# The first head's top-16 search of a PEER layer, with its result handed over in two halves of eight

## What is computed

```python
q = jnp.einsum('nd,de->ne', xb, wq).reshape(blk, PEER_HEADS, 2, PEER_HALF)
s = jnp.einsum('nhcd,hckd->nhck', q, keys).astype(jnp.float32)
sv, si = lax.top_k(s, PEER_TOPK)
cand = (sv[:, :, 0, :, None] + sv[:, :, 1, None, :]).reshape(...)
cidx = (si[:, :, 0, :, None] * PEER_N_KEYS + si[:, :, 1, None, :]).reshape(...)
fs, fpos = lax.top_k(cand, PEER_TOPK)
eidx = jnp.take_along_axis(cidx, fpos, axis=-1)
g = jax.nn.softmax(fs, axis=-1)
act = jax.nn.gelu(jnp.einsum('nd,nhkd->nhk', xb, u_tab[eidx]))
return jnp.einsum('nhk,nhkd->nd', (g * act).astype(xb.dtype), v_tab[eidx])
```

## Time and profile before

| | us |
|---|---|
| median of three runs | 1086.61 |
| the three runs | 1085.2, 1086.61, 1089.31 |
| the profiled execution, its own time | 1081.24 |
| its span, first to last instruction | 1079.6 |
| PE busy | 928.7 (86%) |
| DVE busy | 619.8 (57%) |
| POOL busy | 392.8 (36%) |
| mean granted TensorE clock | 0.978 |

### The profile page before, as it was taken

The page is one execution under the profiler, slowest core; times in us unless marked ns, Lnnn a source line. Parts: engine busy times, 40 slices in busy tenths (PEclk is TensorE's granted clock), DMA queues, the critical chain, the costliest instruction groups (busy, mean ns, idle before and its releaser), DMA issues.

```text
span 1079.6 us, 14164 instructions
## 1 busy us (share of the span) xinstructions
PE 928.7 (86%) x4019; PEld 527.8 (49%) x4019; DVE 619.8 (57%) x1593; ACT 346.6 (32%) x1084; POOL 392.8 (36%) x429
## 2 busy tenths in 40 slices
PE   8999989999999998898998998778757777777775
PEld 6886666665677854455564643223221223322222
DVE  0002266661133879767665776888746677677664
ACT  2223244340001242642433433423312342332432
POOL 3320212222100245553443445445434445445440
PEclk9999999999999999999999999999999999999999
DMA  9984588989984799999999999999979999999994
GB/s 334 327 308 173 210 313 283 311 307 368 351 326 163 287 344 420 416 419 394 415 420 356 400 386 412 421 420 420 415 271 423 422 422 421 422 421 422 420 411 187
DMA packets 76094, 387.61 MB, mean 359 GB/s; under 512 B 11440, under 2 KB 14584, under 8 KB 41912
## 3 DMA queue, kind: packets, MB, share of 16 engines
q0 software_dynamic: 46320, 309.65, 71.2%
q1 hardware_dynamic: 25056, 71.34, 18.5%
q10 hardware_dynamic: 4656, 5.86, 1.5%
HBM read 383.74 MB, written 7.27 MB: 362 GB/s over the span
## 4 chain that ended last, share of the span: by engine, by line
PE 47%; DMA 29%; DVE 8%; issue 8%; ACT 4%; POOL 2%; POOLq 0%; SPq 0%; DVEq 0%; ACTq 0%
DMA big<-peer_uv,idx_r 26%; PE ps L1307 17%; PE ps L890 8%; PE ps L950 4%; PE ps L1198 3%; DVE big L1860 3%; DMA ring<-pack_kv 3%; PE ps L928 3%; POOL big L585 2%; PE ps L1162 2%; PE ps L1271 1%; PE ps L1137 1%; PE ps L1183 1%; ACT wts L784 1%; ACT kv_n L788 1%
## 5 line engine op out<-in xcount | busy, mean ns | idle before, releaser
L1307 PE MATMUL ps<-big,kv_n 128*128 128x512 f32 x1024 | 483.1, 617 | 115.3 <-ACT kv_n L788 115.0
L585 POOL DMA_INDIRECT big<-peer_uv,idx_r x264 | 312.8, 1185 | 356.5 <-PE ps L1307 270.3
L1860 DVE CUSTOM_DVE_ANT_0 big<-big,x_n 128x1024 f32<-128x1024 f32 x256 | 312.1, 1226 | 149.6 <-DMA big<-peer_uv,idx_r 145.9
L1307 PEld LDWEIGHTS ps<-big,kv_n 128*128 128x128 f32 x1024 | 190.2, 195 | 379.9 <-issue 197.1
L778 ACT ACTIVATE gel<-dots 128x2 f32<-128x2 f32 x132 | 26.9, 204 | 365.7 <-DVE dots L1860 365.7
L788 ACT ACTIVATE kv_n<-cst,wts 128x128 f32<-128x128 f32 (+1 forms) x264 | 90.8, 391 | 4.3
L890 PE MATMUL ps<-xT_r,ring 128*128 128x264 f32 x368 | 83.9, 392 | 5.1 <-DMA xT_r<-xT 5.1
L890 PEld LDWEIGHTS ps<-xT_r,ring 128*128 128x128 f32 x368 | 71.1, 194 | 17.5 <-DMA ring<-wall 5.0
L784 ACT ACTIVATE wts<-gk,gel 128x1 f32<-128x1 f32 (+1 forms) x256 | 61.4, 287 | 12.4 <-ACT gel L778 0.4
L1198 PEld LDWEIGHTS ps<-xT_r,ring 128*128 128x128 f32 x512 | 61.2, 191 | 7.4 <-issue 7.4
L1198 PE MATMUL ps<-xT_r,ring 128*128 128x128 f32 (+1 forms) x512 | 64.4, 280 | 0.0
(11 more groups left out here) (346 smaller groups left out, 909.3 us busy)
## 6 DMA issues: line engine op xcount, KB each, us to landing
ring<-wall SPq DMA_DIRECT2D x64, 512.0 KB, 6.6
ring<-pack_kv SPq DMA_DIRECT2D x52, 320.0 KB, 5.0
ring<-pack_kv POOLq DMA_DIRECT2D x44, 320.0 KB, 4.9
big<-pack_cmp POOLq DMA_DIRECT2D x42, 128.0 KB, 3.9
pg_r<-pack_kv SPq DMA_DIRECT2D x16, 320.0 KB, 6.2
pg_r<-pack_kv POOLq DMA_DIRECT2D x16, 320.0 KB, 6.2
big<-peer_uv,idx_r POOLq DMA_INDIRECT x264, 10.5
big<-wall SPq DMA_DIRECT2D x2, 2048.0 KB, 11.6
```

The costliest lines, as they stand in the source:

```text
L585: pool.indirect_dma_start(uv_rows[:, slot, :], None, a["peer_uv"], off).then_inc(uv_in[slot], 16)
L1307: return mm(ps[:, 4 + 2 * tt + c, :], at, row, start=False, stop=stop)
L1860: v.tensor_tensor_reduce(out=uv_rows[:, slot, 0:D], in0=uv_rows[:, slot, 0:D], in1=hrow, scale=1.0, scalar=0.0, op0=ALU.mult, op1=ALU.add, ...
```

## The change

A function `look_up(at, done)` is new. It does what parts 5 to 7 of `find` do, but for eight picks: 12 instructions on half the elements, and then it counts a semaphore up. For head 0 of the first group alone, the search now runs parts 0 to 3, looks up picks 0 to 7 and signals the new semaphore `e0_sb`, then runs part 4 and looks up picks 8 to 15 and signals `e_sb`. POOL's first turn waits for `e0_sb`, its second for `e_sb`. All other heads are as before.

```diff
--- before.py
+++ after.py
@@ -358,6 +358,7 @@
         fsub_sb, gexp_sb, e_sb, hs_out, gs_out, es_out, hrep_in, gks_in, eis_in = (
             sem(n) for n in ("fsub_sb", "gexp_sb", "e_sb", "hs_out", "gs_out", "es_out", "hrep_in", "gks_in", "eis_in"))
         idx_st, idx_go = sem("idx_st"), sem("idx_go")
+        e0_sb = sem("e0_sb")
         uv_in = [sem(f"uv_in{i}") for i in range(SLOTS)]
         dot_sb, v_used, gel_sb = sem("dot_sb"), sem("v_used"), sem("gel_sb")
         ss_out, ss_in = sem("ss_out"), sem("ss_in")
@@ -586,10 +587,16 @@
 
             def rows_of_head(tt, h):
 
-                pool.wait_ge(e_sb, found(tt, h))
+                earliest = isinstance(h, int) and found(tt, h) == 1
+                if earliest:
+                    pool.wait_ge(e0_sb, 1)
+                else:
+                    pool.wait_ge(e_sb, found(tt, h))
 
                 pool.sem_inc(idx_go, 1)
                 for i in range(HEAD_T):
+                    if earliest and i == 1:
+                        pool.wait_ge(e_sb, 1)
                     fetch_turn(h * HEAD_T + (turn0(tt, h) + i), i, eidx[:, tt, bass.ds(h * TOPK + i * SLOTS, SLOTS)])
 
             for tt in range(2):
@@ -1841,6 +1848,24 @@
                     own(v.tensor_copy(eidx[0:r, tt, bass.ds(h * TOPK, TOPK)], w.ea[0:r]))
                     dve.sem_inc(e_sb, 1)
 
+            def look_up(at, done):
+
+                w, n = of_prompt, 8
+                io = cst[:, C_IDX:C_IDX + 16].unsqueeze(1).broadcast_to([P, n, 16])
+                oh = w.oneh[:, 0:16 * n].rearrange("p (k i) -> p k i", k=n)
+                for half in range(2):
+                    if half == 0:
+                        own(TS(w.fi[:, 0:n], w.fpos[:, at:at + n], 4, None, ALU.logical_shift_right))
+                    else:
+                        own(TS(w.fi[:, 0:n], w.fpos[:, at:at + n], 15, None, ALU.bitwise_and))
+                    own(v.tensor_copy(w.fif[:, 0:n], w.fi[:, 0:n]))
+                    own(TT(oh, w.fif[:, 0:n].unsqueeze(2).broadcast_to([P, n, 16]), io, ALU.is_equal))
+                    own(TT(oh, oh, w.idf[:, half:half + 1, :].broadcast_to([P, n, 16]), ALU.mult))
+                    own(v.tensor_reduce((w.ea, w.eb)[half][:, 0:n], oh, AXX, ALU.add))
+                own(STT(w.ea[:, 0:n], w.ea[:, 0:n], 128.0, w.eb[:, 0:n], ALU.mult, ALU.add))
+                own(v.tensor_copy(eidx[:, 0, at:at + n], w.ea[:, 0:n]))
+                dve.sem_inc(done, 1)
+
             def normalise(tt, h, count):
 
                 r, c = (P, 0) if tt < 2 else (ROWS_S, 1)
@@ -1894,8 +1919,11 @@
                      {} if tt else {4: (sc0_sb, h * 2 + 6)} if not isinstance(h, int) or h + 2 < NH else {4: (sc_sb, 32)})
 
             dve.wait_ge(sc0_sb, 2)
-            for part in range(8):
+            for part in range(4):
                 find(0, 0, part)
+            look_up(0, e0_sb)
+            find(0, 0, 4)
+            look_up(8, e_sb)
             gate_sum_others(3, 8)
             own(TS(alpha_id, ident, ALPHA, None, ALU.mult))
             dve.wait_ge(ln_in, 64)
```

## The result

| | before | changed |
|---|---|---|
| median, 8 runs each | 1086.09 us | 1092.48 us |
| lowest, highest | 1083.91, 1091.56 | 1087.82, 1094.66 |
| ratio, 95% interval | | 1.0054 [1.0034, 1.0074] |
| profiled execution, own time (span) | 1081.24 (1079.6) | 1089.34 (1087.7) |
| mean granted TensorE clock, profiled execution | 0.978 | 0.981 |

A forecast was written before the change was run, and what follows sets the result against it. The gather stage, a closed loop that becomes DMA's once started, is started by PE's first sum, which DVE's search and merge tiles make late. Split 2.4 + clock 0.7 = +3.1 us on median 1086.61 gives 1089.7, said 1089.5; range 1085 to 1093.5.

The forecast's parts named there:

- The forecast's own span: The likeliest outcome, slower by 2.4 to 4.1 us with 3.1 in its middle, 1087 to 1092 with scatter; chance 0.68.
- the wide range: Range of the time to hold 8 in 10: 1085 to 1093.5 us.
- the case of over 0.5% slower: Whole kernel slower by over 0.5% (5.4 us), needing extra clock cost or the forecast with scatter; chance 0.10.
- Two of its own signs: L1271 on PE at 366.4 to 367.5; second turn's gathers on POOL 2.4 to 3.5 us later.
- Price of an instruction: Look-up instructions on DVE at half width: 0.16 us for 8 elements, 0.29 for 128.
- The split on DVE: Two look-ups of 3.26 us instead of one of 4.11 cost DVE 2.4 us more ahead of the merge tiles.
- The first gathers: POOL's first gather comes 2.8 us earlier, near 357.6, worth nothing because slots 4 to 7 still wait for L1271.
- The waits of PE: PE idle 3.5 us instead of 1.07 ahead of `other_branch(7)`; a half-speed clock stretch follows, costing 0.7 us.
- Hidden work: ACT's table load and exponential, POOL's wait for `e_sb` before its second copy: all hidden, costing nothing.
- The local sum: On the chain through DVE and PE: 2.4 + 0.7 = +3.1 us, against nothing gained.
- The end: The second turn's delay of 2.4 to 3.5 us is kept as the same distance to the end.
- Rival C: Clock costs more: slow stretch wholly on L1271, 1.7, and another 1.7; +5.8 us with the split's 2.4, 1092.4; chance 0.08.

The follow-up runs named there:

- shifted kernel: Changed kernel with 40 more tiny memsets on DVE earlier, in a stretch where DVE waits for PE: 1091.18 us, ratio 1.0058 [1.0031, 1.0086].
- split without early gathers: Changed kernel, but POOL's first turn waits for `e_sb` again, after both look-ups: 1090.6 us, ratio 1.0048 [1.0028, 1.0068].
- six of padding: Kernel before with six more DVE instructions of 128x256, result unused, ahead of the merge: 1089.49 us, ratio 1.0038 [1.0014, 1.0061].
- gathers early, no second look-up: Changed kernel with the second look-up replaced by a copy of the first one's eight numbers and padding: 1087.44 us, ratio 1.0019 [1.0000, 1.0038].
- PE filled: Changed kernel with 24 more matmul calls, output unread, on PE ahead of `other_branch(6)`: 1090.62 us, ratio 1.0048 [1.0031, 1.0066].
- thirteen of padding: Kernel before with thirteen more DVE instructions of 128x256, result unused, ahead of the merge: 1094.29 us, ratio 1.0081 [1.0050, 1.0112].
- merge first: Changed kernel with merge tiles right behind the first look-up, then part 4, second look-up behind mix tiles 2 and 3: 1091.78 us, ratio 1.0063.
- mix tiles first: Changed kernel with merge tiles, mix tiles 0 to 5 and two dots ahead of the second look-up and head 1's search: 1089.35 us, ratio 1.0043.
- fifth dot in the middle: As mix tiles first, but head 0's fifth dot stands between parts 5 and 6 of head 1's search: 1086.28 us, ratio 0.9984 [0.9965, 1.0002].

## Why the prediction was right, and where it was short

The forecast was slower, by 3.1 us, at 1089.5; measured were 5.9 (3.7 to 8.0) and 1092.48, inside the range and 3.0 above the number. The mechanism held in each of its steps, the size was short. The forecast's own span, +2.4 to +4.1 and 1087 to 1092, ends short of 5.9 and 1092.48. That the wide range holds it owes something to the room left there for a slower clock and for scatter, which is luck as much as foresight. The best estimate, 0.54%, lies even in the case of over 0.5% slower that had 0.10. And +3.1 was said to be less than a measurement could tell, while here the comparison is good to 0.2%. Two of its own signs were missed by a little: the output projection starts at 367.7 by the clock of before (366.4 to 367.5 said), and the second turn's gathers are 3.74 us later (2.4 to 3.5 said).

- **Price of an instruction.** 0.17 and 0.29 us, priced at 0.16 and 0.29. The Trainium skill ("VectorE: DVE Perf Modes", section on the TRN2 errata) gives (N + 151)/0.96 ns for a float32 tensor_tensor, which makes an estimate of 0.29 us for 128 elements. The trace agrees with it (0.29 us at L1862).
- **The split on DVE.** +2.4 predicted, +2.90 in the trace. 0.37 of the difference is the gap behind the first look-up (0.61, where the shifted kernel has 0.24); 0.08 is in two small instructions of the second look-up that took 0.20 and 0.22 instead of 0.17. The gap is the part that was mis-sized: the sum of instructions had no place for it. (The shifted kernel, without the gap, pays about as much at two other places.)
- **The first gathers.** 2.8 us earlier predicted, 2.76 measured, worth nothing that shows. Tried twice, by taking only them away and by keeping only them.
- **The waits of PE.** 3.5 us predicted, 3.97 measured. The slow stretch came where it was expected, 0.51 in 364 to 367.5, and cost the path 0.84 where 0.7 was taken.
- **Hidden work.** ACT's table load, POOL's new wait and the landings stayed off the path, as said.
- **The local sum.** +3.1 predicted, 2.90 + 0.84 = +3.74 measured.
- **The end.** That the distance is kept fits, as far as the scatter lets it be read. At the 17th gather it is 3.75 and 3.63 in the two traces. The 264th gather starts 706.97 to 712.10 behind the search before (three traces, mean 709.8) and 714.22 and 715.04 changed, mean 714.6, which is 4.8 later where single traces of one kernel lie 5.1 apart. The padding shows it by the medians. The 8.1 us between the two profiled executions are 0.90 of an earlier start of the search, 3.74 of the change, and 3.5 that lie within what two traces of the same kernel differ.
- **Rival C** gave 1092.4, the time that was measured, but not by its mechanism. It wanted the slow stretch on L1278, or a second one, or more of them later. In both traces there is one such stretch here, L1278 starts behind it (19.91 and 19.79 us behind the search), and the eight executions had a mean granted clock of 0.9784, beside 0.9785 in the 80 executions of the kernel before that the variants were timed against. The near hit is a coincidence as far as the traces go.

What stays between 3.74 (traces) and 5.9 (ratio): the interval just reaches down to 3.74. The variants lie above their local shift in the same way, by their ratios (split without early gathers 5.2 and 3.45, six of padding 4.1 and 3.04, shifted 6.3 and 3.11). Part of this is the clock of the whole execution. Over the 196 runs here whose clock is known, of all kernels, a line fitted through time against granted clock, with a level of its own for each kernel, falls by 0.55 us (0.46 to 0.65) for each 0.001 of clock, and at equal clock the losses are, with 95% bounds:

| | local shift | loss at equal clock |
|---|---|---|
| changed | 3.74 | 4.8 (3.3 to 6.2) |
| split, gathers late | 3.45 | 3.3 (2.0 to 4.6) |
| gathers early, no second look-up | 0.48 | 1.4 (0.2 to 2.7) |
| PE filled | 3.39 | 4.6 (3.0 to 6.1) |
| six of padding | 3.04 | 3.2 (2.0 to 4.5) |
| thirteen of padding | 7.34 | 6.5 (5.0 to 8.0) |
| shifted | 3.11 | 4.6 (3.2 to 6.0) |
| merge first | 3.09 | 2.9 (1.1 to 4.7) |
| mix tiles first | -2.60, then 2.86 at the 17th gather | 3.2 (1.9 to 4.5) |
| fifth dot in the middle | -2.61, then -1.22 at the 17th gather | 1.0 (-0.2 to 2.3) |

Of the first eight, whose shift is read at the first sum, it lies within the bounds in seven and just outside in one (3.11). So the local shift explains a loss to about 1 us. Whether that last microsecond is something the split does later, or chance, is open.

The version with the mix tiles first fits by its 17th gather. The last one leads there by 1.22 us and shows no gain at equal clock, though its ratio alone (-1.7 us, -3.8 to 0.2) would fit. Whether a lead is handed on as a delay is, stays open. (The executions of the kernel before that stood beside the last version were slower than the others, mean 1087.5 for 1086.0 and 1086.1. Against those alone its figure is 0.5, -0.9 to 1.8.) The fit was made after the runs and is no experiment: a kernel in which PE waits more may itself draw a lower clock.

## What to carry to other kernels

An early hand-over is worth only what its receiver is waited for: here the receiver sat in front of a resource that PE held, and the lead turned into idle DMA. Splitting a step to hand over a half costs its fixed instruction times again, on the engine that does it, so look first who else waits for that engine; if it must be split, put the second half behind all that others wait for, and follow the wait to its next place each time, since it moved twice here (mix tiles, fifth dot). Compare two kernels by distances from a common event in the trace, and leave whole spans to the medians.

## What the runs showed of the hardware

- The same two DVE instructions stood 0.61 us apart in one program and 0.24 us apart when 40 instructions more stood ahead of them in the program; about the same time went into two other instructions, 0.19 us each. Splitting or moving code can thus move some 0.4 us to places that no instruction names.
- A wait of PE of 3.83 to 7.05 us in this stretch was followed by half the granted clock in all six traces that have one (0.51 in 364 to 367.5 of the changed kernel), and with PE busy instead it stayed at 1.00. Gaps of 3.13 and 2.79 us were followed by 0.51 and 0.53 in the kernel before and by 1.00 in the changed kernel. So a trace shows which gap cost clock; its length alone doesn't.
- Granted clock and time go together from run to run of one program: on the changed kernel the two executions at 0.973 took 1092.69 and 1094.66 us, those at 0.985 and 0.981 took 1087.82 and 1089.34 (over its eight runs the correlation is -0.81).
